# VectorE's order of work between two expert blocks: the next block's first multiply ahead of that block's weight differences

## The reference

```python
def _moe(xf, w_router, router_bias, w1, w3, w2):
    ...          # 16 experts of hidden width 512, two per token, from the best group of four
    order = jnp.argsort(flat_e)                      # token places sorted by expert
    ...          # each expert's places are padded to whole blocks of 128 rows
    def expert_block(args):
        xblk, e = args
        return (jax.nn.silu(xblk @ w1[e]) * (xblk @ w3[e])) @ w2[e]

    yb = lax.map(expert_block, (xb.reshape(n_blocks, MOE_BLOCK, D), block_e)).reshape(-1, D)
    y = (yb[dest] * wts.reshape(-1)[order][:, None]).astype(xf.dtype)
    return jnp.zeros_like(xf).at[tok].add(y)
```

## Time and profile before

| what | value |
|---|---|
| median of three runs | 907.03 us |
| profiled execution, its span | 906.41 us, 904.7 us |
| TensorE busy, share of the span | 862.6 us, 95% |
| VectorE busy | 635.5 us, 70% |
| ScalarE busy | 414.9 us, 46% |
| expert blocks 0 to 21 | 458.0 to 867.9 us of the span |
| chain that ended last, shares | TensorE 73%, VectorE 15%, issue 5%, DMA 2% |

### The profile page before, as it was taken

One profiled execution on the slowest core, in us unless ns is written; L12 is line 12 of the kernel. 1 busy time (PEld: TensorE's weight loads), 2 busy tenths in 40 slices (PEclk: granted clock), 3 DMA queues, 4 the chain that ended last, 5 costly groups with the idle time before them and its releaser, 6 DMA issues.

```text
span 904.7 us, 14387 instructions
## 1 busy us (share of the span) xinstructions
PE 862.6 (95%) x4980; PEld 706.6 (78%) x4981; DVE 635.5 (70%) x907; ACT 414.9 (46%) x597; POOL 193.1 (21%) x225
## 2 busy tenths in 40 slices
PE   8999999999999999998889999999999999999983
PEld 7889878888996667887778887877788888877762
DVE  1578756699767657567875587599855746699784
ACT  3584556110226322322515274577543634676672
POOL 4042001100000001101032232224322313242233
PEclk9999999999999999999889999999999999999997
DMA  9954565511044122233966879899989669599974
GB/s 345 342 166 138 162 192 190 156 46 47 1 162 165 70 102 85 95 108 141 364 237 189 286 229 322 257 332 356 353 282 304 211 183 326 170 358 347 345 309 159
DMA packets 115125, 195.27 MB, mean 216 GB/s; under 512 B 4920, under 2 KB 78861, under 8 KB 115083
## 3 DMA queue, kind: packets, MB, share of 16 engines
q1 hardware_dynamic: 103936, 158.87, 51.3%
q0 software_dynamic: 8272, 25.84, 11.2%
q10 hardware_dynamic: 2874, 10.01, 2.8%
HBM read 169.57 MB, written 25.71 MB: 216 GB/s over the span
## 4 chain that ended last, share of the span: by engine, by line
PE 73%; DVE 15%; issue 5%; DMA 2%; DVEq 1%; ACT 1%; POOL 1%; SPq 1%; POOLq 0%; ACTq 0%
PE ps L2390 12%; PE ps L2402 12%; PE ps L2051 9%; PE ps L2054 7%; PE ps L2407 6%; PE ps L2251 2%; PE ps L2384 2%; DMA raw<-in_w_dram 2%; DVE w2l L1817 2%; PE ps L2242 1%; PE ps L2243 1%; PE ps L2244 1%; DVE arena L1833 1%; DVE arena L1386 1%; PE ps L2193 1%
## 5 line engine op out<-in xcount | busy, mean ns | idle before, releaser
L1118 ACT ACTIVATE wah<-raw 128x2048 fp32r (+1 forms) x32 | 61.2, 1915 | 62.3 <-PE ps L2407 47.2
L1817 DVE TENSOR_TENSOR wal<-raw,wah 128x2048 fp32r<-128x2048 f32 x30 | 68.6, 2288 | 27.9 <-ACT wah L1118 27.9
L2390 PE MATMUL ps<-w2h,hTh 128*128 128x512 f32 x184 | 76.0, 413 | 1.2 <-DVE hTl L1828 1.2
L1817 DVE TENSOR_TENSOR wbl<-raw,wbh 128x2048 fp32r<-128x2048 f32 x32 | 73.3, 2292 | 5.1 <-ACT wbh L1118 5.1
L2402 PE MATMUL ps<-wbh,xTh 128*128 128x512 f32 x184 | 74.4, 404 | 0.0
L2402 PE MATMUL ps<-wbl,xTh 128*128 128x512 f32 x184 | 72.4, 394 | 0.0
L2390 PE MATMUL ps<-w2h,hTl 128*128 128x512 f32 x184 | 72.3, 393 | 0.0
L751 POOL DMA_INDIRECT x_rows<-arena,block_dst x21 | 49.9, 2374 | 105.0 <-DVE arena L1833 105.0
L2402 PE MATMUL ps<-wah,xTh 128*128 128x512 f32 x184 | 71.9, 391 | 0.3 <-DVE wal L1800 0.3
L2390 PE MATMUL ps<-w2l,hTh 128*128 128x512 f32 x184 | 72.0, 391 | 0.0
L1817 DVE TENSOR_TENSOR w2l<-raw,w2h 128x2048 fp32r<-128x2048 f32 x32 | 71.7, 2282 | 0.0
(11 more groups left out here) (411 smaller groups left out, 2179.8 us busy)
## 6 DMA issues: line engine op xcount, KB each, us to landing
raw<-in_w_dram SPq DMA_DIRECT2D x64, 1024.0 KB
raw<-in_w_dram SPq DMA_DIRECT2D x16, 2048.0 KB, 11.4
arena<-in_w_mod_dram SPq DMA_DIRECT2D x32, 512.0 KB, 4.0
arena<-in_x_dram SPq DMA_DIRECT2D x16, 512.0 KB, 9.7
arena<-in_w_mod_dram SPq DMA_DIRECT2D x3, 2048.0 KB, 13.7
arena<-in_w_in_dram SPq DMA_DIRECT2D x6, 1024.0 KB, 6.9
x_rows<-arena ACTq DMA_DIRECT2D x9, 512.0 KB, 3.1
hx_rows<-arena ACTq DMA_DIRECT2D x9, 512.0 KB, 4.1
```

Source lines behind the costliest of these rows:

```text
L1118: act.activation(half_of(w_hi[j][:, :], k), half_of(raw[:, bass.ds(base, UNIT)], k), ACT.Copy).then_inc(w_high[j], 1)
L1817: dve.tensor_tensor(half_of(w_lo[j][:, :], k), half_of(raw[:, bass.ds(base, UNIT)], k), half_of(w_hi[j][:, :], k).bitcast(F32), ALU.subtra ...
L2390: ins = pe.matmul(out_ap, parts[l][:, lhs], w_parts[w][:, cols], start=start and n == 0, stop=stop and n == 2)
```

## The change

On VectorE the multiply `hidden(b, 0)` leaves its place inside block b. It is issued at the end of block b-1, as that block's last instruction, behind its `weigh` and its two `w2` low halves and ahead of the loop's branches and of the first `low` of block b. Block 0's stands ahead of the two `w2` low halves of expert 0, and the last block's is issued in block 21, ahead of everything that follows the loop. In a loading block `hidden_low(b, 0)` moves up by one place, from behind the second `wa` low half to behind the first. The number of instructions stays the same. One small product that counts the last block's tokens goes to PSUM bank 4 in place of bank 5, on TensorE and on VectorE.

```diff
             dve.wait_ge(S["g2_loaded"], 16)
+            hidden(0, 0)
             low(2, 2 * UNIT, 0, 0)
             low(2, 2 * UNIT, 0, 1)
             def block(b):
...
                     low(0, place[0] * UNIT, e + 1, 0)
-                    hidden(b, 0)
+                    hidden_low(b, 0)
                     low(0, place[0] * UNIT, e + 1, 1)
-                    hidden_low(b, 0)
                     hidden(b, 1)
                     low(1, place[1] * UNIT, e + 1, 0)
                     hidden_low(b, 1)
...
                     weigh(b)
                     low(2, place[2] * UNIT, e + 1, 0)
                     low(2, place[2] * UNIT, e + 1, 1)
+                    hidden(b + 1, 0)
                 with dve.Else():
-                    hidden(b, 0)
                     hidden_low(b, 0)
...
                     weigh(b)
+                    hidden(b + 1, 0)
...
-            v(dve.tensor_scalar(same_tok, ps[:, 5, 0:P], end_tok_f[:, 0:1], None, ALU.is_equal))
+            v(dve.tensor_scalar(same_tok, ps[:, 4, 0:P], end_tok_f[:, 0:1], None, ALU.is_equal))
...
             dve.wait_ge(S["ss_ready"], SQ + FIN_ORDER.index(ACT_ROW) + 1)
-            hidden(last, 0)
             dve.tensor_tensor(weighted[:, 0:HALF], weighted[:, 0:HALF], nfb[:, 0:HALF], ALU.mult)
...
-            pe.matmul(ps[:, 5, 0:P], ones[:, :], last_diag, start=True, stop=True).then_inc(S["rank_done"], 1)
+            pe.matmul(ps[:, 4, 0:P], ones[:, :], last_diag, start=True, stop=True).then_inc(S["rank_done"], 1)
```

## The result

The changed kernel takes 909.99 us (median of 11 runs, 909.50 to 910.61), the kernel before on the same chip 905.65 us (11 runs, 903.48 to 908.80). The ratio is 1.0044, with a 95% interval of 1.0032 to 1.0057. That is 4.3 us more, outside the 0.3% (2.7 us) that the forecast called no change; the time itself is inside the forecast's own range (905 to 910) and the wider one. The profiled execution takes 910.34 us, its span 908.6.

A forecast was written before the change was run, and what follows sets the result against it. It took VectorE to bound the long runs of loading blocks and TensorE the others, with weight loading a second limit in blocks 18 to 21. Terms -4.95 + 3.0 - 0.4 + 2.8 = +0.45 gave 907.5 us, range 905 to 910.

The forecast's parts named there:

- The sequencer is held: VectorE: a waiting multiply holds the sequencer, so branches and table read come behind the wait instead of running ahead.
- rival 1: VectorE's sequencer isn't held: branches run during the wait, all blocks take 17.74 us, 896 us in all; chance 0.14.
- Block 0: First expert block: the multiply goes ahead of the w2 halves, TensorE's idle time goes, clock stays high; -4.95 us.
- rival 2: Loading blocks: TensorE has more slack before hT_b, odd blocks go through unhindered, blocks cost about 0; 904.3 us, chance 0.14.
- Loading blocks: Blocks loading weights: the wait for hid_a goes, one for hT_b replaces it; +3.0 us in all, bounds 0 to +6.
- Blocks 18 to 21: Late run limited by weight arrival: only the first release counts, about 0.4 us sooner; -0.4 us.
- Behind the loop: After the last loop block: loop exits come behind the wait, TensorE idles some 4.4 us, clock drops; +2.8 us.
- Rival 3: Behind the loop: the clock stays low for longer over the w2 product; up to 910.9 us, chance 0.12.

The follow-up runs named there:

- e6: Changed kernel with the branch and table read of odd blocks ahead of the waiting multiply, even blocks unchanged: 904.81 us, ratio 0.9997 to the kernel before.
- first pair: First profiled executions of the kernel before and the changed kernel, compared block by block; changed kernel's profiled execution 910.34 us, against 906.41 before.
- second pair: One more profiled execution of each unaltered kernel, before and changed, for a second block-by-block comparison; they took 906.85 and 909.57 us.
- e2: Kernel before with the loop's first multiply behind the branches but ahead of its block's first wa low half, hidden_low behind that half: 906.11 us, ratio 0.9997.
- e5: e4 with the last block's multiply back in its old place behind the finished rows: 900.52 us, ratio 0.9954 to the kernel before.
- e3: Kernel before with all multiplies in place and only a bare wait for the next block's Silu ending each block: 968.95 us, ratio 1.0695.
- e10: Changed kernel with one spare VectorE operation (128x512) behind each moved multiply: 909.95 us, ratio 1.0051 to the kernel before.
- e4: Kernel before with block 0's multiply early, others at their block's head behind the branches, the last behind the end tokens: 897.95 us, ratio 0.9903.

## Why the prediction was right or wrong, step by step

**The sequencer is held: right.** The forecast's main choice against rival 1 holds. In the kernel after, L1880's operations come right behind Silu's end (520.64, 520.75); e6 moves only sequencer work and removes the wait in every odd block. The Trainium skill ("Perfetto Trace Analysis", DVE / Act Engine Instruction) has the sequencer ready for the next instruction once one is pushed. For the engine's own queue that fits the `w2` halves; in front of a semaphore that hasn't come, the trace differs here, and the measurement decides. A rival would be that only the loop's waits hold the sequencer, since they take their value from a register. The kernel before speaks against it. Ahead of its loop on ScalarE, a copy (L1130) waits for a fixed value, and the loop's first register operation (L1180) comes next:

```profile
456.63 1.02 ACT L1130 ACTIVATE xTh<-ps 128x1024 fp32r<-128x1024 f32 x1 [1.40 <-PE ps L2384]
L1180 ACTq MOVE  x1: 43/43/43, 456.6 to 456.6; - x1
```

The register operation, which needs nothing, came only when the wait of 1.40 us was over.

**Block 0: right.** -4.8 for -4.95, with no wait for `hid_a` and the clock at 1.00 over the `w2` product (472.2 to 478). The forecast's own terms, 470.44 and 0.42 and 0.14, give 471.00 and so -4.9; other slips of this kind (a first low at 7.57 for 7.59, rival 2 at 904.3 for 904.5) change nothing.

**Loading blocks: right mechanism, one term mis-sized.** The wait for `hid_a` went and one for `hT_b` took its place, in all 15. Predicted was a first low half at a+7.57 in an isolated odd block; it starts at a+8.05 (522.66 less 514.61). The 0.48 between them is the table read, 0.79 where I had taken 0.30 from the kernel before (inside the 1.32 us of the earlier trace rows). From the low half to the fifth group it takes 7.84 (522.66 to 530.50) for my 8.0, so that sum was right. The block becomes 18.7 instead of 18.3, and six of these blocks make +5.2 out of +2.4. In the first pair blocks 4, 6, 8 and 9 came within 0.1 us each of their forecast, with reads of 0.32 to 0.42; block 7, with a read of 0.74, took 18.90 for a forecast 18.54. I had named this error in the bounds ("0.3 us in the first low's start counts in all 11 blocks, so 0 to +6"), and the measured +6.2 and +6.5 of the two pairs lie just beyond that end.

**Blocks 18 to 21: wrong by 2 us, in the good direction.** I counted only the first release, -0.4; measured are -2.5 and -2.7. Block 21 hangs on the arrival of its `wb` weights, and they come sooner than I counted: behind the start of block 18, ScalarE's first copy of them starts at 66.8 us (857.77 less 790.94) where it was 69.7 (858.10 less 788.39); in the second pair it is 66.6 for 69.7. The `wa` copy behaves differently in the two pairs (2.0 us later than in the earlier trace rows in the first, 0.3 us later in the second). Why the `wb` weights come 3 us sooner, and which transfers change places, I didn't settle.

**Behind the loop: right mechanism, undersized.** Predicted was a `w2` product 2.9 us later and +2.8 in all. It starts at 883.77, 15.8 us behind block 22's first matmul, for 12.8 before: 3.0. The idle stretch is 4.40 for the predicted 4.4, and the clock falls as in block 0. But the end moves by 3.8 and 3.6 us in the two pairs. The `w2` product, with the lower clock over its first half, takes 8.0 us for 6.5 before (second pair 7.6 for 6.5). The step that failed is that most of the lower clock's 1.6 us would lie beside the finished rows: of the 1.5 and 1.0 us by which the product grew, 0.8 and 0.7 came through to the end. The chain of waits shows why: after the change it runs through the whole product (883.77 to 891.78), where before it ran through ScalarE's and GpSimd's work on the rows. Rival 3 had the same cause at a larger price (the clock low for the whole product); it was low for about 4 us of it.

**The rivals' prices.** Rival 1's 896 us was wrong as a price too. e2 has almost all its blocks at 17.74 and gains nothing, and e5, with block 0 as well, stops at 900.5. Blocks 7 to 9 and 18 to 21 hang on the weights as soon as VectorE lets them go, and I had priced blocks 4, 7, 8 and 9 by TensorE's 17.74 without asking when their weights would come. Rival 2 (more slack) was wrong: the first low starts later, not sooner.

**The size of the verdict.** My terms sum to +0.45, the profiles' to +2.8 and +2.6 without the stretch ahead of the blocks; the medians differ by 4.3. Runs of the kernel before alone spread from 903.48 to 908.80, so two pairs of profiles can't say what makes the rest. That the total came so near was in part luck: I had the loading blocks some 3.3 us and the end 0.9 us too low, blocks 18 to 21 some 2.2 us too high, and these cancelled in part.

**Open.** Why the table read takes 0.3 us in some blocks and up to 1.9 in others isn't settled. All reads over 0.33 us start 6.3 us or more behind their block's first matmul, where the moved multiply or e3's wait puts them; the reads of the kernel before, 0.5 to 3.5 us behind it, and those of e6's odd blocks are all 0.30 to 0.32. A pause of the sequencer ahead of the read isn't enough: in the kernel before it stood still for 1.7 or 3.6 us, until 0.4 to 1.2 us ahead of each read, too. An empty queue of VectorE is ruled out by e10. The same blocks have the long reads there as in the kernel after (block 7 but not 9 and 10, for instance), so it is no random delay.

## What to carry to other kernels

Before a waiting instruction is moved to the end of a loop body, count the branches, table reads and wait values that come behind it on the same sequencer: in the kernel before they cost nothing, since they ran under earlier engine work; behind the wait they start only at its end. Put the waiting instruction behind the branches instead (e4 does, and at 897.95 us is the fastest version here that loads all its weights). And when the engine that bounds a run of blocks gets faster, ask what the weights' arrival allows before the gain is counted: in e2 it took back all of it.

## What the runs showed of the hardware

- VectorE's sequencer stayed behind an instruction whose semaphore hadn't come, until it came (kernel after: Silu's end 520.64, next branch 520.75), and ScalarE's did the same (kernel before, 456.63).
- A read of one table word into VectorE's sequencer took 0.302 to 0.322 us in the kernel before, and 0.30 to 1.92 us where it came 6.3 us or more behind the block's first matmul (kernel after: median 0.764; e3: up to 1.924).
- The exit of the five empty loop pairs took VectorE's sequencer 3.75 us (874.31 to 878.06), some 0.73 each.
- TensorE's granted clock fell within an idle stretch of 4.4 us (0.83 from 880 to 882, 0.50 from 882 to 884), stayed at 0.50 until 888 and was at 0.96 in the 2 us after that. Behind the idle 2.73 us of e2's block 9 it fell as well (mean 0.93 over the block), behind the 2.80 of its block 20 it didn't (1.00 over the block).
